# Recurrence gates stacked: two passes over rounded and rest part in one set of rows, with ScalarE's and VectorE's orders laid out anew

## What is computed

```
xb = xc.reshape(B, T, LRU_BLOCKS, LRU_BW)
r = sigmoid(einsum("btnc,ncd->btnd", xb, w_gate_a).reshape(B, T, LRU_W) + b_gate_a)
i = sigmoid(einsum("btnc,ncd->btnd", xb, w_gate_x).reshape(B, T, LRU_W) + b_gate_x)
log_a = -LRU_C * r * softplus(-lru_lambda);  a = exp(log_a)
b = sqrt(-expm1(2.0 * log_a)) * (i * xc)
h_t = a_t * h_{t-1} + b_t;   y = h * gelu(g_r)
```

## Time and profile before

| | us |
|---|---|
| median of 3 runs | 2478.1 |
| lowest and highest run | 2477.87, 2479.01 |
| the profiled execution, its own time | 2478.77 |
| its span in the trace | 2477.0 |
| TensorE busy | 2456.6 (99%) |
| VectorE busy | 1801.1 (73%) |
| ScalarE busy | 1220.0 (49%) |
| POOL busy | 516.2 (21%) |

### The profile page before, as it was taken

One profiled execution on the slowest core, in us unless ns is written; L12 is line 12 of the kernel. 1 busy time (PEld: TensorE's weight loads), 2 busy tenths in 40 slices (PEclk: granted clock), 3 DMA queues, 4 the chain that ended last, 5 costly groups with the idle time before them and its releaser, 6 DMA issues.

```text
span 2477.0 us, 43928 instructions
## 1 busy us (share of the span) xinstructions
PE 2456.6 (99%) x17424; PEld 2370.4 (96%) x17424; DVE 1801.1 (73%) x2778; ACT 1220.0 (49%) x2197; POOL 516.2 (21%) x478
## 2 busy tenths in 40 slices
PE   9999999999999999999999999999999999999998
PEld 9999977899999999999999998779999999999997
DVE  8678767579776777677676797674887766776676
ACT  5455355535554554455524643554355544554455
POOL 0024255200112211220201232541001112211222
PEclk9999999999999999999999999999999999999999
DMA  4122201213347635664721222012135456545755
GB/s 157 57 60 73 61 11 38 83 58 107 87 96 136 121 86 103 132 120 90 226 89 52 68 64 61 11 38 96 54 114 104 91 119 131 111 89 113 130 113 172
DMA packets 104537, 230.39 MB, mean 93 GB/s; under 512 B 14816, under 2 KB 17984, under 8 KB 104336
## 3 DMA queue, kind: packets, MB, share of 16 engines
q0 software_dynamic: 43648, 89.14, 20.4%
q1 hardware_dynamic: 60544, 138.42, 17.8%
q10 hardware_dynamic: 144, 0.04, 0.0%
HBM read 144.03 MB, written 81.18 MB: 91 GB/s over the span
## 4 chain that ended last, share of the span: by engine, by line
PE 95%; DVE 3%; issue 1%; DMA 1%; ACT 0%; SPq 0%; DVEq 0%; POOL 0%; POOLq 0%
PE ps L959 27%; PE ps L1353 23%; PE ps L1304 23%; PE ps L1168 5%; PE ps L1183 4%; PE ps L1445 3%; PE ps L1238 2%; PE ps L1416 2%; PE ps L1115 2%; PE ps L1026 1%; PE ps L1140 1%; PE ps L1047 1%; DVE mxp L2519 0%; DVE xall L2778 0%; PE ps L988 0%
## 5 line engine op out<-in xcount | busy, mean ns | idle before, releaser
L2809 DVE TENSOR_TENSOR wlo<-raw_all,whi 128x512 fp32r<-128x512 f32 (+1 forms) x420 | 270.9, 653 | 181.4 <-ACT whi L1974 178.9
L1974 ACT ACTIVATE whi<-raw_all 128x512 fp32r<-128x512 f32 (+1 forms) x420 | 248.7, 600 | 306.5 <-DVE raw_all L2817 106.5
L3308 POOL DMA_DIRECT2D x_scratch<-stage x224 | 199.7, 942 | 842.9 <-DVE stage L2952 698.4
L2027 ACT ACTIVATE stage<-ps 128x536 f32<-128x536 f32 (+1 forms) x224 | 135.5, 612 | 149.4 <-PE ps L1353 143.0
L1497 ACT ACTIVATE whi<-raw_all 128x1024 fp32r<-128x1024 f32 (+3 forms) x72 | 66.6, 926 | 234.0 <-PE ps L959 231.5
L2952 DVE TENSOR_TENSOR stage<-stage,ps 128x536 f32<-128x536 f32 (+1 forms) x168 | 119.0, 708 | 85.7 <-PE ps L1353 84.7
L2519 DVE TENSOR_REDUCE mxp<-ps 64x1 f32<-64x64 f32 (+11 forms) x384 | 140.4, 372 | 54.8 <-PE ps L1115 48.3
L959 PE MATMUL ps<-xgh,whi 128*128 128x358 f32 (+1 forms) x720 | 157.3, 327 | 0.0
L959 PE MATMUL ps<-xgl,whi 128*128 128x358 f32 (+1 forms) x720 | 156.6, 325 | 0.0
L959 PE MATMUL ps<-xgh,wlo 128*128 128x358 f32 (+1 forms) x720 | 156.5, 325 | 0.0
L959 PEld LDWEIGHTS ps<-xgl,whi 128*128 128x128 f32 x720 | 124.0, 189 | 0.0
(11 more groups left out here) (835 smaller groups left out, 7683.0 us busy)
## 6 DMA issues: line engine op xcount, KB each, us to landing
raw_all<-in_wst SPq DMA_DIRECT2D x232, 256.0 KB, 3.4
raw_all<-in_wst SPq DMA_DIRECT2D x80, 512.0 KB, 3.6
x_scratch<-stage POOLq DMA_DIRECT2D x112, 268.0 KB, 5.8
x_scratch<-stage POOLq DMA_DIRECT2D x112, 264.0 KB, 6.1
x_scratch<-xall POOLq DMA_DIRECT2D x24, 537.0 KB, 3.6
xall<-x_scratch SPq DMA_DIRECT2D x24, 537.0 KB, 9.0
xall<-in_xT SPq DMA_DIRECT2D x16, 537.0 KB, 7.4
raw_all<-in_wst POOLq DMA_DIRECT2D x30, 256.0 KB, 4.0
```

The source lines that it names most:

```text
L1974: nc.scalar.activation(dst, src, ACT.Copy).then_inc(S["u_hi"], 1)
L2027: nc.scalar.activation(quarters(stage_of(L, g, i, n)[:, 0:N2]), src, ACT.Copy, scale=-1.0 if row else 1.0).then_inc(S["x_copy"], 1)
L2809: V.tensor_tensor(dst, src, hi.bitcast(F32), ALU.subtract).then_inc(S["u_lo"], 1)
L3308: pool.dma_start(x_scr[2 * i + row, :, a:b], stage_of(L, g, i, n)[:, 0:b - a], accum_op=ALU.add).then_inc(S[done], 16)
```

## The change

A gate's even block (channels 0 to 63 of the 128) and odd block (64 to 127) become two products over 128 rows each. `x_even` holds the hi part of the even block in rows 0 to 63 and its lo part in rows 64 to 127; `x_odd` holds the lo part of the odd block in rows 0 to 63 and its hi part in rows 64 to 127. The weight block holds the 64x64 weights twice, one above the other, for r and i side by side in the output rows. One pass with the weights' hi part and one with their lo part replace the three passes. (The lo x lo term is added by this, too.) The even product goes to banks 6 and 7 and behind the slot's third bank, the odd product to the slot; both form one unit. A gate is then 12 matmuls in place of 18, and there are 57 units in place of 61 in a layer.

`xc_hi` and `xc_lo` become two instructions each over 64 rows. Reading r or i takes three instructions over 64 rows (`gate`). In ScalarE's order `xc_hi(c+1)` moves ahead of `gate_r(c)`. In VectorE's order `xc_lo(c+1)` moves ahead of the next split or behind `gelu`, the eviction of one product moves ahead of `lru(0)` and `lru(1)`, and `lru(2)` moves behind the addition of KR's halves.

```diff
-U_XR, U_GR, U_GATE, U_CKV = [0, 1, 2, 3], [4, 5, 8, 9], [6, 10, 14, 18], [12, 13]
-U_KR, U_CQ = 16, [17, 20, 21, 22, 23, 24]
+U_XR, U_GR, U_GATE, U_CKV = [0, 1, 2, 3], [4, 5, 7, 8], [6, 9, 12, 15], [10, 11]
+U_KR, U_CQ = 13, [14, 16, 17, 18, 19, 20]
...
-    READ[U_GATE[_c]] = ("gate_r", _c + 1)
-    READ[U_GATE[_c] + 1] = ("gate_i", _c + 1)
+    READ[U_GATE[_c]] = ("gate_i", _c + 1)
...
+        x_even, x_odd = xch, xcl
...
+        def even_gates(c, end):
+            rest = ps[:, 3 * slot_of(U_GATE[c]) + 2, CH:CH + end - SUM_END]
+            return (ps[:, 6, :], 0, 512), (rest, SUM_END, end), (ps[:, 7, :], 512, SUM_END)
...
                 def gates(c):
+                    u, b = U_GATE[c], B_GATE[c]
                     w("xc_lo", c + 1)
-                    for k in range(2):
-                        product(to_slot(U_GATE[c] + k), U_GATE[c] + k, B_GATE[c], 128 * k, [tok(xch)], [tok(xcl)])
+                    w("w_lo", b + 2)
+                    take(u)
+                    if c:
+                        w("gate_i", c)
+                    else:
+                        w("root", SUM_MIX)
+                    for i, part in enumerate((whi, wlo)):
+                        for dst, c0, c1 in even_gates(c, TOK):
+                            nc.tensor.matmul(dst, part[b % 2][:, 0:P], x_even[:, c0:c1], start=(i == 0), stop=(i == 1))
+                    for i, part in enumerate((whi, wlo)):
+                        for q in range(3):
+                            mm = nc.tensor.matmul(to_slot(u)(q), part[b % 2][:, P:2 * P], tok(x_odd)(q), start=(i == 0), stop=(i == 1))
+                    mm.then_inc(S["mm"], 1)
...
                 def xc_hi(c):
                     w("conv", c + 1)
                     if c:
-                        w("mm", U_GATE[c - 1] + 2)
-                    nc.scalar.activation(xch[:, :], xc[c][:, :], ACT.Copy).then_inc(S["xc_hi"], 1)
+                        w("mm", U_GATE[c - 1] + 1)
+                    for e, dst in ((0, x_even), (1, x_odd)):
+                        ins = nc.scalar.activation(dst[half(e), :], xc[c][half(e), :], ACT.Copy)
+                    ins.then_inc(S["xc_hi"], 1)
+
+                def gate(c, dst, e, bias):
+                    rest = even_gates(c, T)[1][0]
+                    nc.scalar.activation(dst[0:64, 0:SUM_END].rearrange("p (c n) -> p c n", c=2), ps[half(e), 6:8, :], ACT.Tanh, scale=0.5,
+                                         bias=bias[half(e), c:c + 1])
+                    nc.scalar.activation(dst[0:64, SUM_END:T], rest[half(e)], ACT.Tanh, scale=0.5, bias=bias[half(e), c:c + 1])
+                    return nc.scalar.activation(chunks(dst[64:128, :]), slot(U_GATE[c])[half(1 - e)], ACT.Tanh, scale=0.5, bias=bias[half(1 - e), c:c + 1])
...
-                    nc.scalar.activation(chunks(t1), slot(U_GATE[c]), ACT.Tanh, scale=0.5, bias=half_ba[:, c:c + 1]).then_inc(S["gate_r"], 1)
+                    gate(c, t1, 0, half_ba).then_inc(S["gate_r"], 1)
...
-                    w("mm", U_GATE[c] + 2)
-                    nc.scalar.activation(chunks(t4), slot(U_GATE[c] + 1), ACT.Tanh, scale=0.5, bias=half_bx[:, c:c + 1]).then_inc(S["gate_i"], 1)
+                    gate(c, t4, 1, half_bx).then_inc(S["gate_i"], 1)
...
+                xc_hi(1)
                 gate_r(0)
                 split(8)
                 gate_i(0)
-                xc_hi(1)
...
                 split(13)
+                xc_hi(3)
                 gate_r(2)
                 split(14)
                 gate_i(2)
-                xc_hi(3)
                 split(15)
...
             for s in (0, 1):
                 V.memset(ps[:, 3 * s + 2, CH - 2:CH], 0.0)
+                V.memset(ps[:, 3 * s + 2, CH + TOK - 1024:CH + T - 1024], 0.0)
...
-                    lo(xcl[:, :], xc[c][:, :], xch[:, :], "xc_lo")
+                    V.tensor_tensor(x_even[half(1), :], xc[c][half(0), :], x_even[half(0), :].bitcast(F32), ALU.subtract)
+                    V.tensor_tensor(x_odd[half(0), :], xc[c][half(1), :], x_odd[half(1), :].bitcast(F32), ALU.subtract).then_inc(S["xc_lo"], 1)
...
                 split(7)
+                xc_lo(1)
                 split(8)
-                xc_lo(1)
+                scaled(U_GR[2], g[2], rs, "gr_ev", LIVE)
                 lru(0)
                 split(9)
-                scaled(U_GR[2], g[2], rs, "gr_ev", LIVE)
                 scaled(U_GR[3], g[3], rs, "gr_ev", LIVE)
                 split(10)
                 gelu(0)
+                xc_lo(2)
                 split(11)
-                xc_lo(2)
+                scaled(U_CKV[0], ckv[0][:, 0:T], rs, "ckv_ev")
                 lru(1)
                 split(12)
-                scaled(U_CKV[0], ckv[0][:, 0:T], rs, "ckv_ev")
                 scaled(U_CKV[1], ckv[1][:, 0:T], rs, "ckv_ev")
                 split_kr()
                 gelu(1)
+                xc_lo(3)
                 split(14)
-                xc_lo(3)
-                lru(2)
                 split(15)
                 w("mm", U_KR + 1)
                 w("kr_lo", 1)
                 V.tensor_tensor(chunks(kpe[0:64, :]), slot(U_KR)[0:64], chunks(kpe[0:64, :]), ALU.add).then_inc(S["kr_ev"], 1)
+                lru(2)
                 scaled(U_CQ[0], cq[0], rs, "cq_ev", LIVE)
                 split(16)
                 gelu(2)
```

More of the change, by code:

```diff
@@ L189 @@
 DONE_AT = [CLOSE_DOWN.index((_m, 0)) + 1 for _m in range(8)]
-U_XR, U_GR, U_GATE, U_CKV = [0, 1, 2, 3], [4, 5, 8, 9], [6, 10, 14, 18], [12, 13]
-U_KR, U_CQ = 16, [17, 20, 21, 22, 23, 24]
-U_UQ, U_K, U_V = [25, 26, 27, 28, 29, 30], 31, 35
-U_OY, U_OO, U_MLP = [45 + _c for _c in range(8)], 53, 61
+U_XR, U_GR, U_GATE, U_CKV = [0, 1, 2, 3], [4, 5, 7, 8], [6, 9, 12, 15], [10, 11]
+U_KR, U_CQ = 13, [14, 16, 17, 18, 19, 20]
+U_UQ, U_K, U_V = [21, 22, 23, 24, 25, 26], 27, 31
+U_OY, U_OO, U_MLP = [41 + _c for _c in range(8)], 49, 57
 NU = U_MLP
@@ L244 @@
     LAST_UNIT[B_GR[_c]] = U_GR[_c]
-    LAST_UNIT[B_GATE[_c]] = U_GATE[_c] + 1
+    LAST_UNIT[B_GATE[_c]] = U_GATE[_c]
     LAST_UNIT[B_OO + _c] = U_OO + 2 * _c + 1
@@ L1592, in _ @@
                 split(10)
+                xc_hi(2)
                 gate_r(1)
@@ L1595, in _ @@
                 gate_i(1)
-                xc_hi(2)
                 split(12)
@@ L3387 @@
             put(B_GR[c], block(w_in[:, s3 + P * c:s3 + P * c + P]))
-            gate = np.zeros((P, 2 * P), f32)
-            for n, name in enumerate(("w_gate_a", "w_gate_x")):
-                for i in range(2):
-                    gate[64 * i:64 * i + 64, P * n + 64 * i:P * n + 64 * i + 64] = a[name][l, 2 * c + i]
-            put(B_GATE[c], gate)
+            even = [a[name][l, 2 * c] for name in ("w_gate_a", "w_gate_x")]
+            odd = [a[name][l, 2 * c + 1] for name in ("w_gate_x", "w_gate_a")]
+            put(B_GATE[c], np.tile(np.concatenate(even + odd, 1), (2, 1)))
         for c in range(2):
@@ L3437 @@
         parts = [cols(a["norm_mix_g"][l]), cols(a["q_norm_g"][l]), cols(a["kv_norm_g"][l]), cw, cols(a["conv_b"][l]), cols(a["b_gate_a"][l]),
-                 cols(a["b_gate_x"][l]), cols(a["lru_lambda"][l]), cols(a["attn_out_g"][l]), cols(a["lru_out_g"][l]), cols(a["norm_mlp_g"][l]),
+                 np.roll(cols(a["b_gate_x"][l]), P // 2, 0), cols(a["lru_lambda"][l]), cols(a["attn_out_g"][l]), cols(a["lru_out_g"][l]), cols(a["norm_mlp_g"][l]),
                  cols(a["norm_mix_g"][min(l + 1, DEPTH - 1)])]
```

## The result

The changed kernel takes 2488.97 us (median of six runs, 2485.15 to 2491.29), the kernel before 2478.38 beside it: a ratio of 1.0043, interval [1.0034, 1.0053]. It is 0.43% slower. The forecast had said 2483.4 and a range up to 2487.0. The profiled execution of the changed kernel is the fastest of the six, 2485.15 with a span of 2483.4, that is 6.4 us above the profiled one of before. So there are two things to explain: these 6.4, and the 3.8 by which the median lies higher still.

A forecast was written before the change was run, and what follows sets the result against it. TensorE, busy 99% of the span, was taken to bound the kernel; -0.68 + 3.2 = 2.5 us a layer, twice +5.0, with joints +5.3, on 2478.1 gives 2483.4 us; own range 2481.5 to 2486.5, 8 in 10 2476.0 to 2487.0.

The forecast's parts named there:

- The first path: Gate 2 to CQ1: ScalarE's reads delay CQ0, VectorE's chain through lru(2) delays CQ1; loss 3.2 us a layer, 0.5 to 5.2.
- (1): Before CQ1: POOL misses lru(2), which takes 6.6 us; CQ1 0.5 late against 0.68 gained; 2477.7 us; chance 0.14.
- (2): ScalarE's cost goes by elements, so 64 rows cost half; CQ0 does not wait; 2476.2 us; chance 0.12.
- rival (3): At all gates: the full price of the removed matmuls comes off, 8 x 1.13 = 9.0 us; 2469 us; chance 0.07.
- gates 0 and 1: Next product waits for eviction and split, so only 0.34 of 1.13 us is gained at each, 0.68 for both.
- The range given with the forecast: Whole kernel: 2481.5 to 2486.5 us as the forecast's own range.
- half a microsecond for each of four waits: Allowance in the forecast's own range for the four waits priced from other instructions.
- -0.68 + 3.2 = 2.5 a layer: Each layer: 0.68 us gained behind gates 0 and 1, 3.2 lost before CQ1; 2.5 slower, between -0.2 and 4.5.
- Rival (4): TensorE's clock falls in the new waits, each costing half its length again, 1.4 us, four times; 2489 us; chance 0.05.

The follow-up runs named there:

- fill_kr: Changed kernel with 28 extra matmuls of 128 columns, results unread, behind KR alone in both layers: 2486.42 us, ratio 1.0039.
- xchi_back: Changed kernel with xc_hi(3) back behind gate_i(2) on ScalarE and xc_lo(3) behind the split of block 14 on VectorE: 2489.88 us, ratio 1.0045.
- halves: Changed kernel with a further order like that of reads_first, and the weights' rest part for blocks 7, 10, 16 written in two instructions: 2481.49 us, ratio 1.0019.
- again: The changed kernel rerun with nothing edited, profiled in its longest execution: 2489.74 us, ratio 1.0041.
- reads_first: Changed kernel with both reads of a gate first on ScalarE, Tanh, Exp and Sqrt later, and VectorE's order following: 2483.20 us, ratio 1.0026.
- lru_back: Changed kernel with lru(2) back ahead of the split of block 15 and the addition of KR's halves: 2491.62 us, ratio 1.0051.
- fill: Changed kernel with extra unread matmuls of 128 columns, 28 behind KR and 24 behind gate 3, ahead of the result signals: 2493.92 us, ratio 1.0062.
- both_back: Changed kernel with xc_hi(3) behind gate_i(2), and lru(2) between the split of block 14 and xc_lo(3): 2495.75 us, ratio 1.0066.
- pool_late: Changed kernel with POOL's two GeLU instructions for c = 2 held until the split of block 16 is done: 2491.95 us, ratio 1.0062.
- sum_late: Changed kernel with VectorE's rest part of the sum of squares moved behind the rest parts of the six normed query blocks: 2488.17 us, ratio 1.0036.
- best: The kernel of halves with the one VectorE instruction moved as in sum_late: 2479.08 us, ratio 1.0002.

## Why the forecast fell short

**The first path was right, a little small.** Per layer 2.65 us were forecast at CQ1 and 3.0 came. gate_i ends 13.17 after gate 2 (forecast 12.5): 64-row instructions cost what 128 rows do, as forecast (two are 2.21). Of the 0.67 over, 0.14 lie at the start, 0.19 in xc_hi, 0.21 in the two reads (0.15 had been set aside for them) and 0.12 in the split between them. lru(2) took 9.26 (9.3), with POOL in it as forecast, so rivals (1) and (2) fell; rival (3) fell to the waits. Two errors cancel in part: TensorE runs on 0.05 to 0.14 us after what it waits for, not 0.22, so gates 0 and 1 gained 0.51 each, not 0.34, and TensorE lost 0.53 behind each (2.66 less the gate's 2.13), not 0.8. The range given with the forecast, up to 2486.5, does not follow from half a microsecond for each of four waits, which gives 2481.4 to 2485.4; and the earlier trace rows has a 9 in the last slice too.

**The step that failed is the sum, "-0.68 + 3.2 = 2.5 a layer".** It stopped at CQ1's start, and it held TensorE's clock at full speed throughout: a fall stood outside it, in rival (4) at 0.05. Up to CQ1 the sum was nearly right, and the profiled execution without a fall took 2485.15. In the other profile of the same kernel the clock fell in CQ0, gate 3 came 1.5 and 2.6 us late, CQ1 0 and 0.5, and from CQ1 to the sum behind UQ1 it took 2.6 and 3.2 us longer (layers 0 and 1). For behind CQ1 a second path runs from gate 3: ScalarE's two reads, now three instructions each (two reads 4.96 us in place of 2.3), lru(3), and then VectorE's long order up to the rest parts of the normed queries for UQ0. The trace of before had no wait of TensorE there, and nothing in the prediction asked how near it was to one. All runs together show it (us, layer 0, from starts in the timelines; "tail" is from CQ3's start, behind the sum, to the start of the sum behind UQ1, the product after UQ0):

| kernel | gate 3 after gate 2 | CQ1 after gate 2 | lru(3) after CQ1 | tail |
|---|---|---|---|---|
| before | 23.12 | 26.18 | 7.00 | 54.43 |
| after | 25.20 | 29.99 | 8.60 | 54.69 |
| fill_kr | 25.20 | 29.99 | 8.59 | 54.41 |
| xchi_back | 22.91 | 30.38 | 8.41 | 54.41 |
| halves | 23.19 | 26.77 | 9.81 | 56.97 |
| again | 26.72 | 29.99 | 10.14 | 56.95 |
| reads_first | 22.34 | 26.44 | 10.72 | 56.95 |
| lru_back | 26.83 | 29.41 | 10.90 | 56.96 |
| fill | 25.22 | 30.02 | 11.23 | 56.98 |
| both_back | 27.04 | 31.10 | 11.30 | 56.95 |
| pool_late | 26.69 | 29.43 | 11.97 | 56.98 |
| sum_late | 27.98 | 30.71 | 10.66 | 55.09 |
| best | 23.19 | 26.77 | 9.80 | 55.12 |

Up to 8.6 the tail is that of before within 0.3; from 9.8 on it is 2.5 us longer, unless the sum's instruction is out of the way (the last two rows). Layer 1 shows the same: up to 54.2, then 56.4, and 54.6 in the last two. In the changed kernel the path stands just under that edge, and only because CQ1 itself is late: with CQ1 at 26.18 its lru(3), 38.59 after gate 2, would come 12.4 behind it. Whoever takes away the wait before CQ1 meets the next one, as reads_first and halves did.

The 2.5 us are a step, not a slope, because VectorE then meets POOL's additions. VectorE and POOL in again, at UQ0 (the last VectorE row is the fourth of the four, by itself):

```profile
224.10 1.27 DVE L2250 TENSOR_TENSOR t_r<-t,t_r 128x1074 fp32r<-128x1074 f32 x1
225.29 1.27 DVE L2245 TENSOR_TENSOR cq<-ps,rs 128x1074 f32<-128x1074 f32 x1
226.47 7.57 DVE L2252 SCALAR_TENSOR_TENSOR cql<-cq,vecs,cqh 128x1074 fp32r<-128x1074 f32 x4
230.89 3.16 DVE L2252 SCALAR_TENSOR_TENSOR cql<-cq,vecs,cqh 128x1074 fp32r<-128x1074 f32 x1
...
224.54 2.79 POOL L3205 TENSOR_TENSOR sqa<-sqa,sqa 128x1074 f32<-128x1074 f32 x1 [0.79 <-ACT sqa L1656]
...
230.76 2.15 POOL L3205 TENSOR_TENSOR sqa<-sqa,sqa 128x1074 f32<-128x1074 f32 x1 [2.37 <-ACT sqa L1656]
```

CQ5's eviction starts right behind the sum's instruction, and the four rest parts take 7.57 us. The first meets the end of one of POOL's additions and takes 1.99; the fourth starts 0.13 after the next one and takes 3.16. The same place in the kernel before:

```profile
221.05 1.28 DVE L2217 TENSOR_TENSOR cq<-ps,rs 128x1074 f32<-128x1074 f32 x1 [1.02 <-PE ps L959]
222.34 5.08 DVE L2224 SCALAR_TENSOR_TENSOR cql<-cq,vecs,cqh 128x1074 fp32r<-128x1074 f32 x4
...
227.37 2.88 POOL L3176 TENSOR_TENSOR sqa<-sqa,sqa 128x1074 f32<-128x1074 f32 x1 [4.33 <-ACT sqa L1629]
```

There VectorE had 1.02 us to spare ahead of CQ5's eviction, each of the four took 1.33 or 1.34, and POOL's addition came at their end. And in the changed kernel's first profile, where the clock did not fall:

```profile
223.48 1.28 DVE L2245 TENSOR_TENSOR cq<-ps,rs 128x1074 f32<-128x1074 f32 x1 [0.22 <-PE ps L965]
...
228.77 1.32 DVE L2252 SCALAR_TENSOR_TENSOR cql<-cq,vecs,cqh 128x1074 fp32r<-128x1074 f32 x1
...
229.80 3.11 POOL L3205 TENSOR_TENSOR sqa<-sqa,sqa 128x1074 f32<-128x1074 f32 x1 [3.51 <-ACT sqa L1656]
```

Only 0.22 us were left ahead of the eviction, but the fourth rest part (the second row) still began 1.03 us before POOL's addition.

**Rival (4) came, at a chance of 0.05, by another way.** It foresaw the fall of the clock after the new waits and 2489; the median is 2488.97. That the two numbers meet is luck, for its price, half the wait, four times, was not what happened. Without a fall (the changed kernel's first profile) the time is 2485.15; with falls in CQ0 (again) it is 2491.91, and the 6.7 us between the spans lie mostly behind CQ1: the tail alone is 2.3 and 2.2 us longer. The fall makes gate 3 late, and that tips the second path over its edge. I gave it little because the trace of before showed no wait over 1.0 us; that no row showed a fall was no evidence that there would be none.

The Trainium skill (TensorE: Matmul & The Clock Gate, "HAM oscillation") warned of idle gaps between bursts of matmuls. The traces agree: a fall began in the waits of 4 and 5.2 us (both_back, xchi_back) in both layers, in or behind the wait of 3.0 us before CQ0 in eight of ten cases (two layers of five profiles), behind the wait of 2.5 us before CQ1 in two of four (fill_kr, and not after), and in or behind none of up to 2.1 us (the sum before CQ3 in pool_late the longest).

**Still open**: in how many executions of the changed kernel the clock falls, and for how long. Only the profiled ones show it. That the scatter from 2485.15 to 2491.91 comes from falls in none, one or both layers fits its two ends, and is argued, not shown, in between.

## What to carry to other kernels

When a change makes the results of a step come later on the slower engines, follow them to their last reader, beyond the next product of the engine that sets the end: a path without a wait in the trace before may have only a microsecond to spare, and the profile shows how much in what an engine waits for just ahead of it (here 1.02 us for CQ5). A shorter step on a full engine is worth no more than the work that fits beside it: behind a gate of 2.1 us stood an eviction and a split of 2.4 together, and only halving the split let the gate's whole gain through. And a wait of some 3 us on TensorE should be priced with the clock's fall as the likely case (eight of ten here), and with whom it makes late.

## What the runs showed that was not expected

- The same wait of 3.0 us was followed by no fall of the clock, one of 3.4 us or one of 6.8 us, in executions of the same kernel (after; again, layers 0 and 1).
- Matmuls of 128 columns whose operands never change take 0.115 us each (28 in 3.23 us), over two thirds of the 0.164 of 358 columns.
- A gate of 12 matmuls takes 2.13 us, not 2.05: its even half, four over 512 columns and two over 48, takes 1.15 (133.01 to 134.16), where the like sum product took 1.07. Why was not tried.
